# Expert weights of a float32 transformer kernel in transfers of 2 MiB instead of 1 MiB

## What is computed

```python
def moe_swiglu(h, w_router, w_gate, w_up, w_down):
    ...
    logits = (xf @ w_router).astype(jnp.float32)
    top_logits, top_idx = lax.top_k(logits, TOP_K)          # TOP_K = 2 of N_EXPERTS = 8
    gates = jax.nn.softmax(top_logits, axis=-1)
    ...
    def expert_block(args):
        tok, e = args
        xb = xf[tok]
        hb = jax.nn.silu(xb @ w_gate[e]) * (xb @ w_up[e])   # 1024 -> 3584
        return hb @ w_down[e]                               # 3584 -> 1024
    ...
    y = yb.reshape(n_rows, D).astype(jnp.float32) * row_gate[:, None]
    out = jnp.zeros((T, D), jnp.float32).at[row_tok].add(y)
    return out.astype(h.dtype).reshape(B, S, D)
```

## Time and profile before

| | |
|---|---|
| median of 3 runs | 1912.97 us (1910.3 to 1915.74) |
| profiled execution | 1912.99 us |
| its span, first to last instruction | 1911.1 us |
| busy: PE, DVE, ACT, POOL | 1788.5, 1517.7, 1232.5, 240.0 us |
| memory traffic | 512.04 MB, mean 268 GB/s |
| MoE stage, loads of expert weights | 965.4 to 1885.0 us |

### The profile page before, as it was taken

One profiled execution on the slowest core, in us unless ns is written; L12 is line 12 of the kernel. 1 busy time (PEld: TensorE's weight loads), 2 busy tenths in 40 slices (PEclk: granted clock), 3 DMA queues, 4 the chain that ended last, 5 costly groups with the idle time before them and its releaser, 6 DMA issues.

```text
span 1911.1 us, 23714 instructions
## 1 busy us (share of the span) xinstructions
PE 1788.5 (94%) x8738; PEld 1481.1 (78%) x8738; DVE 1517.7 (79%) x1806; ACT 1232.5 (64%) x1446; POOL 240.0 (13%) x297
## 2 busy tenths in 40 slices
PE   8989998899989899999998999999999999999887
PEld 6867877688878788888887788777777777777666
DVE  7775996858667655454787899989999999999898
ACT  5562135755654454444667688878878888888776
POOL 4113301405011000000007600010001000000000
PEclk9999999999998999999999999999999999999999
DMA  9422334314415245555157999999999999999996
GB/s 352 165 89 82 117 110 182 133 67 176 155 45 218 91 166 187 191 184 195 70 220 273 383 412 421 409 412 422 421 421 380 410 421 422 411 421 421 368 411 282
DMA packets 74297, 512.04 MB, mean 268 GB/s; under 512 B 9392, under 2 KB 9408, under 8 KB 14272
## 3 DMA queue, kind: packets, MB, share of 16 engines
q1 hardware_dynamic: 70736, 498.88, 65.8%
q0 software_dynamic: 3440, 11.58, 2.0%
HBM read 503.08 MB, written 7.36 MB: 267 GB/s over the span
## 4 chain that ended last, share of the span: by engine, by line
PE 40%; DVE 32%; DMA 13%; ACT 8%; issue 4%; POOL 3%; SPq 0%; DVEq 0%; ACTq 0%; POOLq 0%
DVE low L1078 21%; PE psum L1124 15%; DMA raw<-in_moe_weights 12%; PE psum L1518 6%; PE psum L1532 6%; PE psum L1525 6%; ACT high L1075 5%; DVE arena L2257 3%; PE psum L2098 2%; PE psum L1558 1%; PE psum L1563 1%; ACT h L1833 1%; DVE hT_low L4149 1%; POOL places L3622 1%; POOL arena L3627 0%
## 5 line engine op out<-in xcount | busy, mean ns | idle before, releaser
L1078 DVE TENSOR_TENSOR low<-raw,high 128x2048 fp32r<-128x2048 f32 x459 | 1036.4, 2287 | 217.2 <-ACT high L1075 212.9
L1075 ACT ACTIVATE high<-raw 128x2048 fp32r<-128x2048 f32 x459 | 873.7, 1911 | 323.2 <-PE psum L1124 114.9
L1124 PE MATMUL psum<-high,yT_high 128*128 128x512 f32 x776 | 223.9, 396 | 10.1 <-DVE hT_low L4149 3.6
L1124 PE MATMUL psum<-high,yT_low 128*128 128x512 f32 x776 | 219.4, 390 | 0.0
L1124 PE MATMUL psum<-low,yT_high 128*128 128x512 f32 x776 | 213.3, 391 | 0.8 <-DVE low L1078 0.7
L1124 PE MATMUL psum<-low,hT_high 128*128 128x512 f32 x656 | 182.9, 401 | 16.0 <-DVE low L1078 14.8
L1124 PE MATMUL psum<-high,hT_high 128*128 128x512 f32 x656 | 184.1, 403 | 2.0 <-issue 1.5
L1124 PEld LDWEIGHTS psum<-high,yT_high 128*128 128x128 f32 x776 | 142.0, 188 | 40.0 <-issue 6.9
L1124 PEld LDWEIGHTS psum<-low,yT_high 128*128 128x128 f32 x776 | 145.0, 188 | 33.7 <-DVE low L1078 3.3
L1124 PEld LDWEIGHTS psum<-high,yT_low 128*128 128x128 f32 x776 | 145.6, 188 | 31.1
L1124 PEld LDWEIGHTS psum<-low,hT_high 128*128 128x128 f32 x656 | 121.0, 190 | 57.9 <-DVE low L1078 33.3
(11 more groups left out here) (445 smaller groups left out, 2166.4 us busy)
## 6 DMA issues: line engine op xcount, KB each, us to landing
raw<-in_moe_weights SPq DMA_DIRECT2D x336, 1024.0 KB, 10.1
raw<-in_weights SPq DMA_DIRECT2D x132, 1024.0 KB, 4.8
raw<-in_weights SPq DMA_DIRECT2D x2, 896.0 KB, 4.6
raw<-in_weights SPq DMA_DIRECT2D x2, 768.0 KB, 6.3
x<-in_x SPq DMA_DIRECT2D x2, 512.0 KB, 4.0
raw<-in_weights SPq DMA_DIRECT2D x2, 512.0 KB, 3.7
base<-x POOLq DMA_DIRECT2D x1, 1024.0 KB, 6.4
rows<-arena POOLq DMA_DIRECT2D x1, 1024.0 KB, 10.6
```

The lines of the kernel that those rows point to most:

```text
L1075: eng.activation(high, raw, ACT.Copy).then_inc(k.high_ready, 1)
L1078: eng.tensor_tensor(low, raw, high.bitcast(F32), ALU.subtract).then_inc(k.low_ready, 1)
L1124: last = pe.matmul(out, lhs[:, c, :], rhs[:, c, :], start=start and c == 0, stop=stop and c == chunks - 1)
```

## The change

SP issues one transfer for two granules: 2 MiB, 128 rows of 16 KB. It waits for the low part of the later of the two granules that lay in the buffers before. The six buffers of `raw` are the same memory, used as three pairs. ScalarE waits for a landing before the first granule of a pair only. On the host, two granules lie side by side in each row. What ScalarE, VectorE and PE do with a granule, and in which order, stays.

```diff
-def load_expert_part(k, sp, n, expert, part, r=None):
-
-    sp.wait_ge(k.low_ready, granule_number(k, n - RAW, r) + 1)
+def load_expert_parts(k, sp, n, expert, part, r=None):
+
+    assert n % 2 == 0 and part % 2 == 0 and k.first_granule["moe"] % 2 == 0
+    sp.wait_ge(k.low_ready, granule_number(k, n + 1 - RAW, r) + 1)
     slot = (k.first_granule["moe"] + n) % RAW
-    one = k.w["moe_weights"][expert:expert + 1, part] if isinstance(expert, int) else k.w["moe_weights"][bass.ds(expert, 1), part]
-    sp.dma_start(k.raw[:, slot, :], one.rearrange("e p n -> (e p) n")).then_inc(k.landed[slot], 16)
+    w = k.w["moe_weights"]
+    two = w[expert:expert + 1, part // 2] if isinstance(expert, int) else w[bass.ds(expert, 1), part // 2]
+    sp.dma_start(k.raw[:, slot:slot + 2, :].rearrange("p s n -> p (s n)"), two.rearrange("e p n -> (e p) n")).then_inc(k.landed[slot], 16)
...
 def split_expert_part(k, eng, n, r=None):
 
     first = k.first_granule["moe"]
-    if eng is k.nc.scalar:
+    if eng is k.nc.scalar and n % 2 == 0:
...
-        load_expert_part(k, sp, n, expert[t], PLACE_IN_ROUND[kind, j, half])
+        if n % 2 == 0:
+            load_expert_parts(k, sp, n, expert[t], PLACE_IN_ROUND[kind, j, half])
 
     def whole_round(r):
         expert = table_entry(k, sp, r + 1)
-        for i in range(ROUND):
-            load_expert_part(k, sp, i, expert, i, r)
+        for i in range(0, ROUND, 2):
+            load_expert_parts(k, sp, i, expert, i, r)
...
-    weights = np.zeros((N_EXPERTS, ROUND, P, GRANULE), np.float32)
+    weights = np.zeros((N_EXPERTS, ROUND // 2, P, 2 * GRANULE), np.float32)
...
-            weights[e, i] = packed(block)
+            weights[e, i // 2, :, GRANULE * (i % 2):GRANULE * (i % 2 + 1)] = packed(block)
```

## The result

| | before | with the change |
|---|---|---|
| median | 1912.63 us (4 runs, 1910.3 to 1915.74) | 2015.22 us (4 runs, 2013.77 to 2016.94) |
| ratio | | 1.0534, 95% interval 1.0517 to 1.055 |
| forecast | | 1926, range 1902 to 1953 |

The account below looks back on a forecast made before the run. DMA transfers were taken to set the pace in the MoE stage. Stops 12.8, small lags 5, longer rows -5.6 and the end 1 summed to +13.2 us on 1912.99, giving 1926.2 us, range 1902 to 1953.

Parts of the forecast that it names:

- the stops: Three places in the MoE stage where ScalarE waits long for TensorE; DMA engines would idle there, +12.8 us.
- the budget before: Six buffers turn in 14.9 us: 4.5 landing to issue, 10.4 issue to landing, 4.7 needed, so 5.7 us slack.
- the slack of 1.0: With three pairs, compute engines may run 1.0 us late per 14.9 us turn before the DMA engines run dry.
- Calm stretches: Two long MoE stretches, 600 us together, where transfers set the pace; they should not lose.
- rival (c): Calm stretches leak: every second pair needs 8.1 against 7.7 us, 24 us more, 1950 us; chance 0.13.
- The walk: Ten granules followed through ScalarE's and VectorE's order: longest pair 7.5 us from landing to issue, 7.7 allowed.
- Small lags: Twelve other 25 us stretches between 1100 and 1900 us with low issue-to-landing minimum: +5 us, bounds 0 and 8.1.
- Rows of 16 KB: Longer rows may speed expert loads: gain between nothing and 11.2 us, half taken, -5.6 us.
- The end: The last pair lands as one, so its first low part is done later: +1 us, from 0 to 2.2.
- The costs of nothing: Fewer SyncE issues, ScalarE landing waits left out and first pairs loaded early: no effect on time.
- (a): Longer rows win: rate goes to 429 GB/s, the stops lose nothing, 1902 us; chance 0.25 with its neighbours.
- (b): Nothing moves: compute engines must catch up after a stop, so lost stock costs nothing, 1914 us; chance 0.20.

Follow-up runs that it names:

- 5 single: Kernel before, each load waiting so that five single 1 MiB buffers are in use instead of six: 1935.77 us, ratio 1.0121.
- 4 single: Kernel before, each load waiting so that four single 1 MiB buffers are in use instead of six: 2039.17 us, ratio 1.0668.
- 4 pairs: The change with a fourth pair of buffers in arena space free in the MoE stage, used from the 17th pair on: 1909.41 us, ratio 0.9976.
- 3 pairs, short low parts: The change with VectorE's low parts of expert weights cut to 64 of 2048 columns, ScalarE's high parts in full: 1904.64 us, ratio 0.9954.

## Why the prediction was wrong

**Direction.** Slower was forecast with 0.55 and came. The size was wrong by a factor of about eight, outside the range. That the direction came out right is partly luck: the term that gave it, the stops, is there, but some 70 of the 103 us arose where the forecast had put nothing.

**What bounds the kernel, the budget before.** Right: transfers set the pace, and the six buffers' turn, 4.5 us of landing to issue and 10.4 us of issue to landing, stands.

**The step that failed** is "of these 10.4 only 4.7 are needed", and with it "the transfer of two granules needs 4.7 + 2.48 = 7.2 us" and the slack of 1.0. The minimum of the trace is the time of a load that meets an empty queue. It says how long such a load takes, not that a stream of them keeps the rate. What a stream needs is seen where a run leaves less time (all in 1150 to 1400 us, with ScalarE's high parts in full):

| run | time left, median us from issue to landing | GB/s |
|---|---|---|
| 6 single (before) | 10.3 | 417 |
| 5 single | 7.9 | 412 |
| 4 single | 7.2 | 364 |
| 4 pairs | 12.5 | 423 |
| 3 pairs, short low parts | 10.5 | 420 |
| 3 pairs (the change) | 10.0 | 370 |

So a granule needs about 7.9 us for next to the full rate, and a pair about 10.5; both are estimates, since only these steps were run, and the rates contain the lags of the compute engines (without them 7.3 us gave 386 GB/s). Set into the forecast's own account, the kernel before had 10.4 - 7.9 = 2.5 us of slack, not 5.7, and the change has 14.9 - 6.7 - 10.5 = -2.3, not 1.0: it was 2.3 us short before any lag. That the change takes 4.7 us of slack was right; what it was taken from was not. The same account puts the other runs in their order: about 0 us of slack with only the issue in pairs, only the landing in pairs, or five buffers (1929, 1934 and 1936 us), -2.5 with four single buffers (2039 us) and +2.7 with four pairs (1909 us).

**Calm stretches, forecast 0, and rival (c), 24 us.** The walk was right in what it walked (7.5 us from landing to issue at most was forecast; a turn with a small expert's step shows 7.8), but it was held against the wrong limit. The rate there fell from 418 and 417 to 372 and 373 GB/s. 600 us at 417.5 GB/s become 672 at 372.5: some 72 us of the 103. Rival (c) had the place right and put it down to the 0.4 us of a coincidence; it was given 0.13 and a third of this size.

**Stops, forecast 12.8.** The mechanism is shown: with 2.5 us less slack the share at the second stop falls by 0.12 of 25 us, 3.0 us. In the change the second and third stop cost about 3 us more each. At the first the share of 50 us is 0.93 now, 0.04 under the level of 0.97, and was 1.00, 0.01 under the level of 1.01: 1.5 us more. Together that is some 8 us, not 12.8, partly because the level they fall from is lower. **Small lags, forecast 5:** not measured apart. What is left beyond calm stretches and stops, some 23 us, lies in the rest of the stage, of which the forecast took nothing: its first part, where the traffic fell as well (1100 to 1150 us: 413 GB/s before, 369 now), and the last steps.

**Rows of 16 KB, forecast -5.6.** With a full queue the change's transfers give 428 against 421 GB/s, close to the upper end of 429; rows and transfer size are not told apart. The taking of half was harmless; the gain does not show in the change, whose queue is not full. The 10.2 us that the forecast worked out from the packet floor of the Trainium skill (DMA: Bandwidth & Descriptors, Bandwidth) and left aside lie closer to the measured 1.7% of 600 us.

**The end, +1.** From the issue of the last load to the end of the span the kernel took 1911.1 - 1885.0 = 26.1 us and takes 2015.0 - 1983.9 = 31.1 now. The last load carries two granules now, and the last granule used to be issued one granule later, so some 2.5 of these 5.0 us are not a loss; the rest is a little more than the forecast's upper bound of 2.2. **The costs of nothing:** nothing in the runs speaks against them; none was measured alone.

**Rivals (a) and (b).** (a) fails with the same step: it held the queue to be full enough. (b) held that lost slack costs nothing; with five single buffers 2.5 us of it cost 21.7 us. What should have been doubted is a slack taken from a minimum. The trace of before had the warning: in its two calm stretches no load landed less than 8.0 us after its issue, so there was no row that said what the rate is at 7 or 8 us, and the range had to take in that it might be lower.

**What stays open.** Why a stream with 2 MiB ahead of each load does not get the full rate is not settled. The share per byte is higher: 0.99 at 386 GB/s with three single buffers, 1.01 at 417 with four, 6% more for a byte, so the packets are recorded as longer; what they wait for is not seen. Beside that there are short gaps. The share of the DMA engines in the changed kernel, in tenths, 0.25 us for each digit, from 1626 to 1636 us:

```profile
DMA  9997996969765984158967999399975999986991
```

At 1630.0 us it is down to 0.1, though two pairs are outstanding, one issued at 1622.0 that lands at 1631.6 and one issued at 1628.4 that lands at 1638.2. So engines stand idle while transfers are in flight, and an average of 0.97 hides it. A guess that would fit is that some of the 16 engines run dry while others still have work, which a deeper queue would hide; no view here separates the engines, and it is not shown.

## What to carry to other kernels

A buffer's budget has two halves, and the transfer's half is not the shortest landing of the trace: it is the issue-to-landing time at which the rate is still full, and here only runs with less time showed it. Merging buffers in pairs takes from both halves at once, a later free buffer and a later first use; either alone cost 1%, both together 5%. Before merging, ask what a load has ahead of it when it is issued, in bytes; longer rows in larger transfers are worth 1.7% here, and only with a queue that stays full.

## What the hardware showed that was not expected

- The rate depends on how much is outstanding at issue, well above one transfer: 357, 386 and 417 GB/s with 1, 2 and 3 MiB ahead, while the DMA share is 0.94, 0.99 and 1.01. A share of 0.96 to 0.99 is no sign of full rate: the change had 0.97 at 373 GB/s. With 2 MiB ahead in one pair instead of two granules it is 384.
- Transfers to partitions 0 to 63 and then 64 to 127, 1 MiB each with rows of 16 KB, at a mean share of the 16 engines of 1.00, move 222 GB/s over 750 us, about half of what transfers over all 128 partitions do.
- Rows of 16 KB go as one packet each (128 packets fewer for a pair than rows of 8 KB). Together with transfers of 2 MiB in place of 1 MiB they save 41 ns for each MiB with a full queue.
